# First modulation vector on TensorE, and a value projection that takes its input block by block, in a two-block transformer kernel

## What is computed

```python
c_act = jax.nn.silu(c)                                     # (1, 1024)
mod = jnp.einsum('bd,de->be', c_act, w_ada[l]) + b_ada[l]  # (1, 6 * 1024)
shift1, scale1, gate1, shift2, scale2, gate2 = jnp.split(mod, N_MOD, axis=-1)
hmix = modulate(rmsnorm(x, g_norm1[l]), shift1, scale1)    # h * (1 + scale) + shift
proj = jnp.einsum('bsd,de->bse', hmix, w_in[l])
sb_q, sb_k, sb_v, r_q, r_k, r_v, r_g, br = jnp.split(proj, IN_SPLITS, axis=-1)
```

## Time and profile before

| | |
|---|---|
| median of 3 runs | 2107.85 us (2107.8 to 2108.03) |
| profiled execution, span | 2108.7 us |
| PE busy | 2042.7 us, 97% of the span |
| DVE, ACT, POOL busy | 940.0, 892.0, 895.8 us |

### The profile page before, as it was taken

The page is one execution under the profiler, slowest core; times in us unless marked ns, Lnnn a source line. Parts: engine busy times, 40 slices in busy tenths (PEclk is TensorE's granted clock), DMA queues, the critical chain, the costliest instruction groups (busy, mean ns, idle before and its releaser), DMA issues.

```text
span 2108.7 us, 27749 instructions
## 1 busy us (share of the span) xinstructions
PE 2042.7 (97%) x9940; PEld 1680.5 (80%) x9940; DVE 940.0 (45%) x1168; ACT 892.0 (42%) x1094; POOL 895.8 (42%) x412
## 2 busy tenths in 40 slices
PE   5999999999999999999999999999999989999998
PEld 3788877878788887888888878778898778888887
DVE  6055541454545453611112336877572257555313
ACT  3366663232323233423232346678553335444321
POOL 1422214434343334344444446759265134444443
PEclk7999999999999999999999999999999999999999
DMA  7311102524242422233333322220144122333231
GB/s 284 100 51 60 61 21 90 203 87 168 76 169 75 169 70 90 71 109 99 96 93 100 108 92 75 75 71 2 60 133 138 50 80 80 100 99 99 94 106 60
DMA packets 57261, 203.75 MB, mean 97 GB/s; under 512 B 6240, under 2 KB 8416, under 8 KB 56928
## 3 DMA queue, kind: packets, MB, share of 16 engines
q1 hardware_dynamic: 57184, 202.70, 29.5%
HBM read 200.57 MB, written 2.10 MB: 96 GB/s over the span
## 4 chain that ended last, share of the span: by engine, by line
PE 74%; issue 8%; DVE 6%; ACT 6%; POOL 5%; DMA 1%; SPq 0%; POOLq 0%; DVEq 0%; ACTq 0%
PE acc L1973 17%; PE acc L1975 17%; PE acc L1974 17%; PE aux L1973 5%; PE aux L1975 5%; PE aux L1974 5%; POOL w_lo L483 3%; ACT sp L540 2%; POOL cfy L506 2%; PE acc L2209 2%; PE aux L2107 1%; DVE qkvf L1646 1%; PE aux L2110 1%; PE aux L2199 1%; PE aux L2122 1%
## 5 line engine op out<-in xcount | busy, mean ns | idle before, releaser
L483 POOL TENSOR_TENSOR w_lo<-raw,w_hi 128x1024 fp32r<-128x1024 f32 x321 | 781.4, 2439 | 1158.3 <-ACT w_hi L540 1157.3
L540 ACT ACTIVATE w_hi<-raw 128x1024 fp32r<-128x1024 f32 x321 | 339.5, 1060 | 571.6 <-PE acc L1975 411.3
L1973 PE MATMUL acc<-x_hi,w_hi 128*128 128x512 f32 (+1 forms) x1336 | 526.7, 394 | 11.6 <-DVEq L1120 4.7
L1975 PE MATMUL acc<-x_hi,w_lo 128*128 128x512 f32 (+1 forms) x1336 | 518.1, 388 | 0.0
L1974 PE MATMUL acc<-x_lo,w_hi 128*128 128x512 f32 (+1 forms) x1336 | 518.1, 388 | 0.0
L1973 PEld LDWEIGHTS acc<-x_hi,w_hi 128*128 128x128 f32 x1336 | 251.8, 189 | 69.6 <-DVEq L1120 8.5
L1975 PEld LDWEIGHTS acc<-x_hi,w_lo 128*128 128x128 f32 x1336 | 251.6, 188 | 51.8
L1974 PEld LDWEIGHTS acc<-x_lo,w_hi 128*128 128x128 f32 x1336 | 252.1, 189 | 49.7 <-issue 0.5
L1151 DVE SCALAR_TENSOR_TENSOR adac<-ada,c_act,adac 128x1024 f32<-128x1024 f32 x42 | 61.3, 1459 | 91.5 <-DMA ada<-in_ada 90.5
L1419 DVE TENSOR_TENSOR ht<-acc,tn 128x512 f32<-128x512 f32 x21 | 14.5, 691 | 173.8 <-PE acc L1975 171.3
L1973 PE MATMUL aux<-w_hi,x_hi 128*128 128x512 f32 x192 | 76.2, 397 | 3.3 <-DVE x_lo L1176 2.0
(11 more groups left out here) (490 smaller groups left out, 3611.6 us busy)
## 6 DMA issues: line engine op xcount, KB each, us to landing
raw<-in_weights SPq DMA_DIRECT2D x324, 512.0 KB, 3.6
ada<-in_ada SPq DMA_DIRECT2D x32, 512.0 KB, 3.5
ada<-in_ada SPq DMA_DIRECT2D x8, 1024.0 KB, 10.0
resid<-in_x SPq DMA_DIRECT2D x1, 2048.0 KB, 9.3
out<-resid SPq DMA_DIRECT2D x16, 128.0 KB, 1.7
decay<-in_tables SPq DMA_DIRECT2D x4, 256.0 KB, 3.5
memf<-in_mem SPq DMA_DIRECT2D x1, 1024.0 KB, 4.9
angles<-in_tables SPq DMA_DIRECT2D x1, 512.0 KB, 3.8
```

The source lines that it names most:

```text
L483: nc.gpsimd.tensor_tensor(w_lo[s][:], raw[s][:], w_hi[s][:].bitcast(F32), ALU.subtract).then_inc(lo_ready, 1)
L540: return nc.scalar.activation(out, in_, func, **kw)
L1973: M(out, a_hi, b_hi, start=first, stop=False)
L1975: return M(out, a_lo, b_hi, start=False, stop=last)
```

## The change

Eight things are changed, all of them ahead of tile 8 (the first query tile):

1. The first third of w_ada is stored anew in the input array `ada_first`: load k brings, for feature block k alone, all 1024 rows of scale and shift (128x8x256 floats, still 1 MB).
2. `c_act` is written into column 0 of `c_pad` (8 blocks of 128x32, the rest zero). `modulation_rows(k)` multiplies on PE: eight fp32 matmuls with 32 stationary and 256 moving columns. Their outputs go to four groups of 32 partitions, d % 4.
3. DVE copies the 128x256 result (`take_rows`), PE adds its 128 partitions with two one-column matmuls (`modulation_sums`), and DVE makes one column of `gain1` and `mod` (`modulate`, three operations on 128x1). The 16 operations on 128x1024 are gone, and so are the 16 one-column matmuls.
4. So block k of the normalised input needs load k alone, not all eight.
5. The value projection goes block by block over six banks (all four token groups of the first 512 values, two groups of the second 512): 18 matmuls for each k. Two banks remain and are done after all k, from units that are kept in `vw_hi` and `vw_lo`. The units of the two halves are interleaved in HBM.
6. Five fp32 products of the ones with the tables, whose result nobody reads, stand on PE: two ahead of the squares, one at the fifth square, two ahead of block 0.
7. SP's queue: `small` and x in two halves first, then `cols`, then w_ada loads and weight units in turn; `halves` last.
8. ACT makes `c_act` between the fourth and the fifth square; it makes `w_hi` of two units ahead of every second `x_hi`.

```diff
+            def take_rows(k):
+                own["ada_rows_done"].next()
+                own["ada_used"].at = own["ada_used"].at + 1
+                ins = V.tensor_copy(ada_rows[:, k % 2, :], rows_home(k))
+                ins.then_inc(S["ada_used"], 2)
+                own["ada_used"].next()
...
             for k in range(KT):
-                dve.wait_ge(S[f"ada0_loaded{k % 4}"], 16 * (k // 4 + 1))
-                for m in (1, 0):
-                    own["ada_used"].own(ada(ada0[:, 2 * (k % 4) + m, :], adac0[:, m, :], k))
...
+                own["normed"].own(V.scalar_tensor_tensor(tn[:, k % 2, :], resid[:, k, :], gain1[:, k:k + 1], rs,
+                                                         ALU.mult, ALU.mult))
+                if k + 2 < KT:
+                    take_rows(k + 2)
+                low(k)
+                if k + 2 < KT:
+                    modulate(k + 2)
...
+            def modulation_rows(k):
+                pe.wait_ge(S[f"ada0_loaded{k % 4}"], 16 * (k // 4 + 1))
+                if k >= 2:
+                    pe.wait_ge(S["normed"], k - 1)
+                out = rows_home(k)
+                for d in range(KT):
+                    g = 32 * (d % 4)
+                    m = M(out[g:g + 32, :], c_pad[:, d, :], ada0[:, k % 4, d, :], start=d < 4, stop=d >= 4,
+                          skip_group_check=True)
+                m.then_inc(S["ada_rows_done"], 1)
...
+            for n in range(2):
+                M(aux[:, 2 * T:3 * T], ones, small[:, 0:T], start=True, stop=True)
             for k in range(KT):
                 own["rsq_ready"].next()
+                if k == KT // 2:
+                    M(aux[:, 2 * T:3 * T], ones, small[:, 0:T], start=True, stop=True)
                 m = M(rs, ones, x_sq[:, k, :], start=k == 0, stop=k == KT - 1)
+                if k == KT // 2:
+                    own["c_ready_act"].next()
+                    modulation_rows(0)
             m.then_inc(S["stat_ready"], 1)
-            own["ada_used"].next(2 * KT - 1)
-            modulation(adac0[:, 1, :])
-            own["ada_used"].next()
-            modulation(adac0[:, 0, :], 1)
-            token_tiles(At(0), (0, 1, 2, 3), ready=own["x_ready"])
+            modulation_sums(0)
+            modulation_rows(1)
+            modulation_sums(1)
+            for n in range(2):
+                M(aux[:, 2 * T:3 * T], ones, small[:, 0:T], start=True, stop=True)
+            v_banks = [aux[:, b * T:(b + 1) * T] for b in range(NB)] + [bank(At(0)), bank(At(1))]
+            for k in range(KT):
+                if k + 2 < KT:
+                    modulation_rows(k + 2)
+                own["x_ready"].next()
+                for n, out in enumerate(v_banks):
...
+                    m = three(out, x_hi[:, k, b * P:(b + 1) * P], x_lo[:, k, b * P:(b + 1) * P],
+                              hi_home(u)[:, cc], lo_home(u)[:, cc], k == 0, k == KT - 1)
...
+                    if n == 0 and k + 2 < KT:
+                        modulation_sums(k + 2)
```

More of the change, by code:

```diff
@@ L424, in load, with load_ada @@
                 sp_.dma_start(raw[s][:], src).then_inc(raw_loaded[s], 16)
[L426 to L430, removed]
+            def load_ada(k):
                 if k >= 4:
                     sp_.wait_ge(S["ada_used"], 2 * (k - 3))
[L433 to L436, removed]
+                sp_.dma_start(ada0[:, k % 4, :, :], dram["ada_first"][k]).then_inc(S[f"ada0_loaded{k % 4}"], 16)
+            half = KT // 2
+            sp_.dma_start(small[:], dram["small"]).then_inc(S["tables_loaded"], 16)
+            sp_.dma_start(resid[:, 0:half, :], dram["x"][:, 0:half, :]).then_inc(S["x_loaded"], 16)
+            sp_.dma_start(resid[:, half:KT, :], dram["x"][:, half:KT, :]).then_inc(S["input_loaded"], 16)
+            sp_.dma_start(cols[:], dram["cols"]).then_inc(S["consts_loaded"], 16)
+            load_ada(0)
+            load(At(0))
+            load(At(1))
+            load_ada(1)
+            load_ada(2)
+            load(At(2))
+            load(At(3))
+            load_ada(3)
+            load_ada(4)
+            load(At(4))
+            load(At(5))
+            load_ada(5)
+            load_ada(6)
+            load(At(6))
+            load(At(7))
+            load_ada(7)
+            sp_.dma_start(halves[:], dram["halves"]).then_inc(S["decay_loaded"], 16)
             def load_units(first, end):
@@ L564, in roots, with norm_hi @@
                 done.own(f(dst, sums, ACT.Exp, scale=-0.5))
[L566 to L570, removed]
+            def norm_hi(k):
+                own["normed"].next()
+                own["norm_hi"].own(f(x_hi[:, k, :], tn[:, k % 2, :], ACT.Identity, bias=mod[:, k:k + 1]))
             def last_square(src, u):
@@ L584, in scaled_tile @@
                     own["rsq_used"].next(2)
-            act.wait_ge(S["consts_loaded"], 48)
-            own["c_ready_act"].own(f(c_act[:], cols[:, C0["c"]:C0["c"] + KT], ACT.Silu))
             act.wait_ge(S["x_loaded"], 16)
             for k in range(KT):
+                if k == KT // 2:
+                    act.wait_ge(S["consts_loaded"], 16)
+                    step.own(f(c_act[:], cols[:, C0["c"]:C0["c"] + KT], ACT.Silu))
+                    own["consts_ready"].next()
+                    own["c_ready_act"].own(f(c_pad[:, :, 0], c_act[:]))
+                    act.wait_ge(S["input_loaded"], 16)
                 own["rsq_ready"].own(f(x_sq[:, k, :], resid[:, k, :], ACT.Square))
@@ L1167, in _ @@
[L1167 to L1188, removed]
@@ new lines, in low @@
+            def low(k):
+                own["norm_hi"].next()
+                own["x_ready"].own(V.scalar_tensor_tensor(x_lo[:, k, :], tn[:, k % 2, :], mod[:, k:k + 1],
+                                                          x_hi[:, k, :].bitcast(F32), ALU.add, ALU.subtract))
+            for k in range(2):
+                take_rows(k)
+                modulate(k)
+            own["rs_ready"].next()
+            for k in range(KT):
+                own["normed"].own(V.scalar_tensor_tensor(tn[:, k % 2, :], resid[:, k, :], gain1[:, k:k + 1], rs,
[5 more added lines that the diff above has]
+                    modulate(k + 2)
@@ L1243, in _ @@
             own["v_ready"].next(8)
+            own["tile_done"].skip(2)
             qk_low(At(0), qt_hi, qt_lo, SC)
@@ L2071, in _, with modulation_sums @@
+            def modulation_sums(k):
+                own["ada_used"].next(2)
+                out = sums_home(k)
+                for n, m_ in enumerate((1, 0)):
+                    m = M(out[:, n:n + 1], ada_rows[:, k % 2, m_ * P:(m_ + 1) * P], ones[:, 0:1], start=True, stop=True)
+                m.then_inc(S["ada_ready"], 1)
+            pe.wait_ge(S["tables_loaded"], 16)
+            for n in range(2):
+                M(aux[:, 2 * T:3 * T], ones, small[:, 0:T], start=True, stop=True)
             for k in range(KT):
@@ L2080, in _ @@
+            for b in (2, 3):
+                for k in range(KT):
+                    cc = slice(k % 2 * T, (k % 2 + 1) * T)
+                    m = three(aux[:, (2 + b) * T:(3 + b) * T], x_hi[:, k, b * P:(b + 1) * P], x_lo[:, k, b * P:(b + 1) * P],
+                              vw_hi[:, k // 2, cc], vw_lo[:, k // 2, cc], k == 0, k == KT - 1)
+                m.then_inc(S["tile_done"], 1)
             own["v_ready"].next(2)
-            token_tiles(At(4), (4, 5, 0, 1))
             tile(At(8), At(0), x_hi, x_lo)
```

103 lines of the change are left out of this document (68 added, 35 removed).

## The result

The change made the kernel slower: 2114.6 us (median of 13 runs, 2111.05 to 2117.39) beside 2108.38 us for the kernel before (13 runs, 2107.66 to 2113.57). The ratio is 1.0023, with an interval of 1.0015 to 1.0031. The prediction was 2102.5, with a range of 2098.5 to 2110: faster was expected, and slower came. The profiled execution has a span of 2110.5 us and was timed at 2112.3, so it is one of the quicker ones.

The account below looks back on a forecast made before the run. DMA was taken to bound the prologue, then PE and DVE work, with PE what the end waits for. Tile 8: 25.2 + 5 x 7.3 + 4.7 + 19.1 = 85.5 against 90.84, 5.3 us earlier: 2102.5 us, range 2098.5 to 2110.

Parts of the forecast that it names:

- full clock from 12 us to 290: Sign to look for on PE: clock up by 12.65 us in the prologue, value matmuls in the loop at 0.228 us.
- The clock falls in the loop: Rival, 0.13: PE's 1.5 us waits per block lower the clock; 2.8 us a fall, five falls give 2116.5.
- the waits that did bring it down left PE busy a third of the time, these leave it over half: Argument against clock falls in the loop, from the wait near 302: PE busy 1.04 of 3 us, then half clock.
- I cost them at nothing: Loop: ACT (0.72 us an `x_hi`, 2.1 two units) and POOL (2.4 a unit) have room within the 7.3 us block.
- three DVE operations of 0.2 each: Prologue, after sums 1 (0.45 us): DVE's small operations, done at 21.6, ahead of `tn` of block 0.
- the prologue hangs on `cols`: Prologue: `cols` lands at 10.2, fifth square done at 12.65; not the eight loads set the start, 25.2.
- A set of rows at 1.05 us: `modulation_rows` on PE: 0.85 us with four column groups at once, plus 0.2 for start and switch.
- Rows overlap less: Rival, 0.15: two groups at a time, 0.85 us more per set, 2109.3; no overlap (within it, 0.03) 2123.
- The copy at 0.43: DVE's copy of the 128x256 rows, in prologue and loop: 0.43 us, between 0.69 and 0.42 of other operations.
- The block at 7.3: Loop, blocks 0 to 4: 7.3 us each, 3.2 of them not value matmuls, 1.5 idle PE.
- That the wait for free banks goes: Value projection: the 1.31 us wait for free banks goes away, as six banks are empty.
- The gain from spared falls: Behind tile 8: where a wait lies may save or cost 1 to 2 us by the clock; left at nothing.

Follow-up runs that it names:

- e2: The change with pairs of fp32 products with a zero stationary filling PE's waits for `x_lo` in the loop: 2106.91 us, ratio 0.9985.
- e5: The change with `x_lo` ahead of the copy of the rows, and the gain in one DVE operation reading PSUM: 2098.74 us, ratio 0.9946.
- e8: e5 with the first two weight units rounded before the root, while ACT waits for the sums: 2093.99 us, ratio 0.9927.
- e1: The change with DVE making `x_lo` of block k before it copies the rows of k + 2: 2099.82 us, ratio 0.9956.
- e3: The change with the gain made in one DVE operation that reads its sum from PSUM, one plus bias made once: 2112.68 us, ratio 1.0013.
- e6: The kernel before with unread products, 13 behind the sums of squares and two behind the one-column ones: 2106.07 us, ratio 0.9986.

## Why the prediction was wrong

Tile 8 was forecast at 85.5 and came at 94.96, 9.5 us later. By blocks, against 7.3 us each (0 to 4) and 23.8 for all after: the start +1.2, block 0 +3.7 (11.02), block 1 0.0 (7.31), block 2 +0.4, block 3 +2.0, block 4 +0.4, the rest +1.8 (25.6). By causes: 6.5 for the clock and 3.2 for POOL's hold (both below), 0.4 with no cause shown, less some 0.6 that the prologue was quicker elsewhere.

**The step that failed is the clock in the loop.** The sum took every value matmul after block 0 began at 0.228 us, and expected "full clock from 12 us to 290". The case that happened is the rival *The clock falls in the loop*, which had 0.13. Its price, 2.8 us for a fall of 14 matmuls, was nearly right for the first (some 3.1) and too high for the next two (1.6 and 1.8, for 8 and 9 matmuls); together 6.5 from the blocks, 6.8 by e2. (The other 0.4 of block 3 lies between PE's rows, begun at 58.76, and the copy at 60.41: 1.65 us, where the other blocks have 1.24. No run shows why.) What was wrong is the argument against it, that "the waits that did bring it down left PE busy a third of the time, these leave it over half". Waits of 1.4 to 2.0 us, each with a microsecond of rows ahead of it, did bring it down, three times in the profiled execution. The earlier trace rows had one example of a fall and none of where the limit lies; an argument from one such row deserved even chances. The Trainium skill, "TensorE: Matmul & The Clock Gate" ("HAM oscillation"), says that idle gaps of a few microseconds in a loop lower the clock; here gaps of 2.0 us and less did.

**The second step is "I cost them at nothing", said of ACT and POOL in the loop,** and with it "three DVE operations of 0.2 each" in the prologue, which took no notice of POOL. POOL was in time, but held DVE up: 1.8 us in the gain of block 1 (1.96 for 0.16), on the path to the first value matmul, and 0.6, 0.4 and 0.4 in three `x_lo`. That is where the 0.4 in blocks 2 and 4 come from, and 0.6 of block 0. The Trainium skill, "SBUF — State Buffer" ("Who interferes with whom"), states the rule: DVE shares a pair of ports with GpSimd, and an operation of DVE with two SBUF inputs contends with a GpSimd operation that reads SBUF; either can be the one that is blocked. The trace agrees (1.96 beside 0.16 us, 2.96 beside 0.75 in e5 against e8, and POOL's unit of 2.82 beside 2.36). A sign of it stood in the kernel before: POOL's first unit, at 34.45, took 2.90 us, and the next two some 2.3 each, while DVE's last operation on `adac` ran until 35.13. The prediction did not look for it.

**What was right.** That the prologue hangs on `cols`; the order of the steps in it (25.2 forecast; 26.36 measured, with 1.8 too little for the hold and some 0.6 too much elsewhere, as `cols` landed at 9.6 and load 0 at 12.1 instead of 10.2 and 12.8). A set of rows at 1.05 us: 1.0 measured, so the rival *Rows overlap less* falls. The copy at 0.43 (0.42). The block at 7.3 (7.31), with idle time of 1.5 (1.43). That the wait for free banks goes.

**What lies behind tile 8.** The gain from spared falls was priced at "1 to 2 us"; the rest took 2015.5 instead of 2017.9 us, 2.4 less, and between 2015.1 and 2016.9 in all versions of the change. One place of it is a stop of 1.94 us that both kernels have. PE's timeline of the kernel before, then of the change:

```profile
1381.89 0.50 PE L1973 MATMUL acc<-x_hi,w_hi 128*128 128x512 f32 x1 [1.94 <-DVEq L1120]
...
1384.30 0.63 PE L1975 MATMUL acc<-x_hi,w_lo 128*128 128x512 f32 x1
1384.73 0.63 PE L1973 MATMUL acc<-x_hi,w_hi 128*128 128x512 f32 x1
```

```profile
1385.11 0.50 PE L2023 MATMUL acc<-x_hi,w_hi 128*128 128x512 f32 x1 [1.94 <-DVEq L1164]
...
1387.06 0.40 PE L2025 MATMUL acc<-x_hi,w_lo 128*128 128x512 f32 x1
1387.29 0.39 PE L2023 MATMUL acc<-x_hi,w_hi 128*128 128x512 f32 x1
```

Behind the same stop the clock falls before and stays up in the change, so that the 24 matmuls there take 5.59 us instead of 7.22. And the fall near 305 of the earlier trace rows lasts some 6.7 us before and 3.4 in the change. So the first slice is not the only place with the lower clock, as the text on the profile before has it: that trace has it near 305, 1383 and 1728 us too.

So 4.1 us lost at tile 8 are 1.8 in the span (2110.5 against 2108.7). The timed runs lose more, 0.23% or 4.9 us by the ratio. They spread over 6.3 us, those of the kernel before over 5.9, and e1's, with no fall in the loop, over 2.0 in five runs. The mean granted clock is known for each run: 0.992 or 0.993 in the change's three quickest, 0.989 in its four slowest. So slower runs spend more time at the lower clock; whether in the loop or behind it only the profiled execution shows, and this stays open. So does how much the 0.2 us of one-column work in each block adds to what the waits do.

## What to carry over

When a change cuts a long phase into pieces with a short wait in each, price the clock as well as the waits: five waits of 1.4 to 2.0 us cost 9 us in themselves and 6.8 more in falls. Ask of each wait whether what stands ahead on the releasing engine is needed by the waiting one; here a copy for the block after next stood ahead of `x_lo`, and two lines in the other order were worth some 14 us (the ratio went from 1.0023 to 0.9956), 13.2 of them by the start of tile 8. And where GpSimd works on long operations, list the DVE operations with two SBUF inputs that can meet them: freeing one of them moved the hold to the next (e3), and moving GpSimd's first two units freed the last one that PE waited for (e8).

## What the runs showed of the hardware

- An operation of DVE with two SBUF inputs that meets one of GpSimd ends with it (128x1: 22.75 beside 22.73) or, at 128x512, some 0.55 us after it (36.77 to 37.33; 25.07 to 25.62 in e5; 42.57 to 43.13 in e6). Size hardly matters: 0.16 us of work became 1.96. Where DVE gets in between two units, the second one waits (2.82 instead of 2.36 us at 51.73).
- Sixteen fp32 passes of 256 columns on four column groups take 1.0 us, beside an estimated 3.4 one after the other at full clock (16 x 0.213, half of the 0.43 of 512 columns in the earlier trace rows): all four groups run at once.
- A PE that counts as busy can have the clock fall under it: in e6 it was at full speed when 32 passes with one moving column began and fell 2 us later. A wait of 1.76 us stood ahead of them, and no run parts the two.
